# Moving the weight and token blocks of a Trainium2 transformer kernel to other starts within their 64-byte lines

## The chip, the cores and the metric

One core of one Trainium2 chip runs the kernel. The metric is the device time of one execution in microseconds (us); less is better.

## The reference

The reference is two transformer blocks on 512 tokens of width 1024 in float32. The first is a mixer (eight heads of forgetting attention beside four heads of gated linear attention), a cross attention to 256 memory tokens and an MLP of width 4096. The second has a gated MLP (ffn1), a token mixer with differential and block-sparse attention, and another gated MLP (ffn2). Cut to what matters here:

```python
def rms_norm(x, g):
    return x * rsqrt(mean(x * x) + EPS) * g
u = relu(rms_norm(h, norm_mlp_g) @ mlp_w1)          # the MLP: 1024 -> 4096 -> 1024
h = h + (u * u) @ mlp_w2
...
def swiglu(h, w1, w3, w2):                          # ffn1 and ffn2: 1024 -> 2816 -> 1024
    return (silu(h @ w1) * (h @ w3)) @ w2
x = x + 0.5 * swiglu(rmsnorm(x, ffn1_norm), w1, w3, w2)
```

## The kernel before

Every matrix product works on float32 values that are split into a high and a low part (names that end in `h` and `l`). One product is three matmuls: high by high, high by low, low by high. All activations lie transposed on chip, 128 partitions by tokens. A matmul has a stationary operand (128 columns, loaded first by a weight load) and a moving operand that streams through it.

Two kinds of dense work exist. A **panel** (`panel_t`, `chunks` and their kin, lines 975 to 977) takes 256 columns of a weight matrix for the whole depth of 1024. SyncE loads it into `raw`, ScalarE copies its high part into `wh`, VectorE subtracts the low part into `wl`. Its matmuls mostly stream 512 tokens, held in `xh`/`xl` or `ah`/`al`. The **products by sevens** do a part of the MLP and most of ffn1 and ffn2 with Strassen's scheme: a weight matrix and the tokens are cut into quarters, sums of quarters are formed, and seven block products take the place of eight. One block product is 24 matmuls (2 halves of columns, 4 slices of depth, 3 matmuls) with 256 moving columns each, accumulated in one bank. In the MLP it is the function `groups` (lines 1530 to 1532), in ffn1 and ffn2 the function `stream` (lines 1550 to 1552). TensorE runs them back to back in a fixed order; ScalarE, VectorE and the DMA queues prepare blocks ahead.

In these products the stationary operand is a weight block and the moving operand a token block:

- Weight blocks lie in halves of the sides of `wh`/`wl` (1024 floats each). In the MLP the slots 4 and 5 lie in the four quarters of `xh`, which holds no panel's tokens then (`parts_of`). In ffn1 and ffn2 a ring of five blocks is used (`ring_at`): four in `wh`/`wl`, and one, `RING_h`/`RING_l`, at the start of the arena.
- Token blocks are `XS_h`/`XS_l`, seven blocks of sums of the normed tokens in the arena, when the product goes up to the hidden width. When it goes down again (`DOWN`), they are the hidden values `US` in `xh`, `xl`, `ah`, `al` (`hidden_at`).

The arena is one large tensor, `arena` (and `arena_r`, the same bytes in the matmuls' type), in which the stages lay out what they need; the attentions' operands lie there too. Tensors are allocated one after another, so a tensor's length decides where the next one begins. In the built program the byte addresses within a partition are: `h` 2,176, `xh` 18,560, `xl` 34,944, `ah` 51,328, `al` 67,712, `raw` 84,096, `wh` 100,480, `wl` 116,864, `cst` (constants, with the identity matrix for transposes) 133,248, and `arena` 149,024. All but the arena's are multiples of 64; the arena begins 32 bytes past one. Slices of depth, halves of columns and blocks are multiples of 512 bytes apart, so a block's start tells the place in its line of all its matmuls.

Of the kernel before, what the change touches and what calls it, by code (L numbers as in the profile page):

```python
# [8 lines left out]
F32R = mybir.dt.float32r  # L9
AX = mybir.AxisListType  # L10

PART = 128
T, M, D = 512, 256, 1024
KT = D // PART
PC = 256
QT = T // PART
HALF = 64
D_FF, D_FF2 = 4096, 2816
CMP_L, CMP_S = 32, 16
NCMP = (T - CMP_L) // CMP_S + 1  # L20
# [7 lines left out]
W1_COL, at = {}, 0  # L28
# [3 lines left out]
W2_COL, at = {}, 0  # L32
# [5 lines left out]
P0, at = {}, 0  # L38
# [28 lines left out]
ROWS, at = {}, 0  # L67
# [40 lines left out]
HT = KT // 2  # L108
NETS = ["mlp", "ffn1", "ffn2"]
MLP_G = 6  # L110
PHASES, at = {}, 0
# [195 lines left out]
def constants():  # L307
# [4 lines left out]
    def put(name, a):  # L312
        nonlocal at
        a = np.asarray(a, np.float32).reshape(PART, -1)
        where[name] = at
        at += a.shape[1]
        parts.append(a)
# [13 lines left out]
    put("cmpany", (valid.any(-1)).astype(np.float32).T)  # L331
    put("tril", (p[:, None] % HALF) <= np.arange(HALF)[None, :])
    put("chunk", np.tile(np.arange(T)[None, :] % HALF != 0, (PART, 1)))
    put("block", (p[:, None] // HALF) == (p[None, :] // HALF))
    inv = (np.float32(1.0) / (np.float32(10000.0) ** (np.arange(0, HALF, 2, dtype=np.float32) / np.float32(HALF)))).astype(np.float32)
    ang = (np.arange(T, dtype=np.float32)[:, None] * inv[None, :]).astype(np.float32)
    put("cos", np.cos(ang).T[p % (HALF // 2)])
    put("sin", np.sin(ang).T[p % (HALF // 2)] * np.where(p % HALF < HALF // 2, -1.0, 1.0)[:, None])
    sel = np.zeros((PART, 4))
# [29 lines left out]
def build(nc, d, out):  # L369
    ctx = ExitStack()  # L370
    with ctx:
        def sb(name, shape, dt=F32):
            return ctx.enter_context(nc.sbuf_tensor(name, shape, dt))
# [6 lines left out]
        xh_at = -(-nc.sbuf_base // 32) * 32  # L380
        xh = sb("xh", [PART, KT, T], F32R)
        xh_f = nc.alloc_sbuf_tensor_at("xh_f", [PART, 4, HT, PC], F32, offset=xh_at)
        xl_at = -(-nc.sbuf_base // 32) * 32
        xl = sb("xl", [PART, KT, T], F32R)
        xl_f = nc.alloc_sbuf_tensor_at("xl_f", [PART, 4, HT, PC], F32, offset=xl_at)
# [4 lines left out]
        al = sb("al", [PART, KT, T], F32R)  # L390
        al_f = nc.alloc_sbuf_tensor_at("al_f", [PART, 4, HT, PC], F32, offset=al_at)
        raw = sb("raw", [PART, 2, KT, PC])
        wh = sb("wh", [PART, 2, KT, PC], F32R)
        wl = sb("wl", [PART, 2, KT, PC], F32R)
        cst = sb("cst", [PART, CONSTS.shape[1]])
        gT = sb("gT", [PART, NROWS])
        foxb = sb("foxb", [8, 1])
# [12 lines left out]
        std4 = sb("std4", [PART, QT])  # L410
        idle = sb("idle", [PART, 8])
        AW = 19936
        arena_at = -(-nc.sbuf_base // 32) * 32
        arena = sb("arena", [PART, AW])
        sm_h, sm_l = (x[:, 0, 0:KT * SMALL].rearrange("p (k n) -> p k n", k=KT) for x in (ah, al))
        arena_r = nc.alloc_sbuf_tensor_at("arena_r", [PART, AW], F32R, offset=arena_at)

        class Arena:
# [5 lines left out]
            def __call__(self, *shape):  # L424
                n = int(np.prod(shape))
                assert self.at + n <= AW, (self.at, n)
                v = self.store[:, self.at:self.at + n]
# [74 lines left out]

        A = Arena()
        N_sq, N_acc, N_dg = A(2, T), A(T), A(QT, PART)
        N_end = A.at
        F_out = A(KT, T)
        O_nat = A(QT, D)

        A = Arena()
        SM, PB, PTs = A(2, T), A(2, 2, T), A(2, T)  # L510
        att_end = A.at

        A = Arena(1024)
        A(T)
        X_h1, X_h2, X_std, X_inv, X_rs = (A(QT, 16) for _ in range(5))
        A = Arena(3072)
        H_sq = A(2, T)
        X_l = SM[0:16, 0, :]
        A = Arena(att_end)
# [13 lines left out]
        A = Arena(16300)  # L533
        G_dec = A(2, T // HALF)
        A = Arena()
        G_kn, G_at, G_S, G_sq = A(2, 2 * PART), A(2, 2, 2 * HALF), A(2, PART), A(4, PART)
        A = Arena(2048)
# [7 lines left out]
        A = Arena(att_end)  # L545
        A = Arena(att_end + 2 * T)
        M_sq, M_acc, M_dg = A(2, M), A(M), A(2, PART)
        N_rsm = M_sq[:, 0, :]
        A = Arena(att_end)
# [4 lines left out]
        A = Arena(16316)  # L554
        C_r2, C_ms, C_inv, C_rq, C_nrq = A(QT), A(QT), A(QT), A(4 * QT), A(4 * QT)

        A = Arena(N_end)
        XS_h, XS_l = (Arena(N_end + e * 7 * HT * PC, arena_r)(7 * HT, PC).rearrange("p (b k) n -> p b k n", b=7) for e in range(2))
        A = Arena(N_end + 2 * 7 * HT * PC)
        E_t, E_u, P_F = A(2, T), A(2, T), A(2, T)  # L560
        P_T = Arena(0)(4, PC)
        RING_h, RING_l = (Arena(e * HT * PC, arena_r)(HT, PC) for e in range(2))
        U_T = P_F.rearrange("p a n -> p (a n)").rearrange("p (a n) -> p a n", a=4)
        E_tl, E_tr, E_ul, E_ur = (e[:, c, :].rearrange("p (a n) -> p a n", a=2) for e in (E_t, E_u) for c in range(2))
        LEFT, RIGHT = slice(0, PC), slice(PC, T)
# [1 line left out]
        A = Arena(att_end)  # L567
# [12 lines left out]
        D_t = A(2, T)  # L580
        assert A.at <= AW, A.at

        S_x2 = arena[:, D_q[1].offset % AW:D_q[1].offset % AW + 4 * T].rearrange("p (a n) -> p a n", a=4)
        S_bf, S_kr, S_kraw, S_vT = SM, PTs, PB[:, 0], PB[:, 1]
        S_gT = D_on[:, 0].rearrange("p a n -> p (a n)")
        S_hT = D_on[:, 1].rearrange("p a n -> p (a n)").rearrange("p (a n) -> p a n", a=2)
        w2_at = D_V[1].offset % AW
        A = Arena(w2_at)
        S_w2k, S_w2v, S_h1 = A(2, PART), A(2, HALF), A(2, 2, 2 * NCMP)

        A = Arena(mix2_at)
# [29 lines left out]
        def parts_of(g, a):  # L621

            (net, r), i = PHASE_OF[g]
            slot = SLOT[PHASES[net, r][0], 7 * i + a]
            if slot < 4:
                return tuple(x[:, slot // 2, slot % 2 * HT:(slot % 2 + 1) * HT, :] for x in (wh, wl))
            x = xh.rearrange("p k n -> p (k n)").rearrange("p (b k n) -> p b k n", b=4, k=HT)
            return x[:, 2 * (slot - 4)], x[:, 2 * (slot - 4) + 1]

        def banks(g):  # L630

# [46 lines left out]
        def own(name):  # L678

            return (P0[name] + 10) % 2  # L680
# [9 lines left out]
        def ring_at(name, b):  # L690

            at = b % RINGS
            if at == 0:
                return RING_h, RING_l
            side = own(name) if at < 3 else 1 - own(name)
            at = (at - 1) % 2
            return tuple(x[:, side, at * HT:(at + 1) * HT, :] for x in (wh, wl))

        def landing(name, s, n):

# [269 lines left out]
        def _(pe):  # L970
# [542 lines left out]
            def groups(key):  # L1513

                g0 = PHASES[key][0]
                for i, n in TURN[key]:
                    g = g0 + i
                    a, b, at = PRODUCTS[n]
                    o = banks(g)[at].rearrange("p (f n) -> p f n", f=2)
                    (left_h, left_l) = parts_of(g, a)  # L1520
                    pe.wait_ge(st_l, high_count(g, a))
                    if n in (2, 4, 5):
                        pe.wait_ge(st_e, 3 * g + {2: 1, 4: 2, 5: 3}[n])
                    elif n == 6:
                        pe.wait_ge(st_c, 3 * g + 2)
                    for c in range(2):
                        cols = slice(c * PART, (c + 1) * PART)
                        for k in range(HT):
                            begins = n in (0, 1, 3) and c == 0 and k == 0
                            nc.tensor.matmul(o[:, c, :], left_h[:, k, cols], XS_h[:, b, k, :], start=begins, stop=False, skip_group_check=True)  # L1530
                            nc.tensor.matmul(o[:, c, :], left_h[:, k, cols], XS_l[:, b, k, :], start=False, stop=False, skip_group_check=True)
                            mm = nc.tensor.matmul(o[:, c, :], left_l[:, k, cols], XS_h[:, b, k, :], start=False, stop=k == HT - 1, skip_group_check=True)
                    mm.then_inc(st_q, 1)
# [343 lines left out]
        def _(act):  # L1877
# [458 lines left out]
            def block_high(g, a):  # L2336

                (net, r), i = PHASE_OF[g]
                g0, _, p = PHASES[net, r]
                n = 7 * i + a  # L2340
                if a in (A11, A12, A22):
                    act.wait_ge(st_r[buffers(g)], 48 * len(same_buffers(g)) + 48)
                else:
                    act.wait_ge(st_a, sum_count(g, SUM[a]))
                if n >= RING:
                    act.wait_ge(st_q, 7 * g0 + n - RING + 1)
                elif SLOT[g0, n] >= 4:
                    act.wait_ge(lin_done, 2 * (p - 4))
                else:
                    act.wait_ge(lin_done, 2 * (p - 1 if SLOT[g0, n] // 2 == p % 2 else p))  # L2350
                nc.scalar.activation(parts_of(g, a)[0], raw_of(g, BUF[a]), ACT.Copy).then_inc(st_h, 1)
# [434 lines left out]
        def _(dve):  # L2786
# [543 lines left out]
            def block_low(g, a):  # L3330

                dve.wait_ge(st_h, high_count(g, a))
                if a in SUM:
                    dve.wait_ge(st_a, sum_count(g, SUM[a]))
                to_h, to_l = parts_of(g, a)
                low(to_l, raw_of(g, BUF[a]), to_h, st_l)
# [711 lines left out]
```

## Time and profile before

| | |
|---|---|
| time before | 2123.26 us, median of 3 runs (2122.52 to 2123.94) |
| time of the profiled execution | 2123.62 us |
| its span, first to last instruction | 2121.8 us |
| TensorE busy | 2103.8 us (99%) |
| VectorE busy | 1399.6 us (66%) |
| ScalarE busy | 1053.1 us (50%) |
| granted TensorE clock | 1.000 of full speed |

The span is what the trace covers; the time of the execution is 1.82 us longer. Durations of matmuls overlap (one fills the array while the last one drains), so the pace of TensorE is not its duration of about 0.28 us but the distance from one start to the next. The timeline gives starts to 0.01 us, and 24 of them tell the pace of one block product.

### The profile page before, as it was taken

How to read it: one execution, taken by the hardware profiler on the slowest of the kernel's cores; microseconds unless marked ns; L12 is line 12 of the kernel's file. 1: busy time of each engine (PE TensorE's matmuls, PEld its weight loads, DVE VectorE, ACT ScalarE, POOL GpSimd, SP SyncE). 2: the span in 40 equal slices, each digit the busy share in tenths (PEclk: the TensorE clock that was granted, in tenths of full speed). 3: DMA queues.
4: the chain of work that ended last, by engine and by line, in shares of the span. 5: the costliest groups of instructions: out<-in, count | busy, mean ns of one | idle time of the engine just before them, and what ended most of it. 6: DMA issues, size and time to landing. Idle time of an engine off the chain costs nothing.

```text
span 2121.8 us, 33199 instructions
## 1 busy us (share of the span) xinstructions
PE 2103.8 (99%) x13292; PEld 1816.3 (86%) x13292; DVE 1399.6 (66%) x2337; ACT 1053.1 (50%) x1762; POOL 52.0 (2%) x68
## 2 busy tenths in 40 slices
PE   9999999999999999999999999999999999999999
PEld 7888988888998988899988888887777888899997
DVE  4664663467665767688856777647776357678874
ACT  6664545443533543464543565546667234445454
POOL 0000000000000011110100000000000000000000
PEclk9999999999999999999999999999999999999999
DMA  5121522156355366875543522321111233345432
GB/s 191 60 81 61 192 94 72 40 149 189 102 167 145 94 160 173 229 204 159 142 137 102 179 85 81 99 85 51 27 50 33 88 99 95 104 126 154 129 91 79
DMA packets 210827, 243.83 MB, mean 115 GB/s; under 512 B 9953, under 2 KB 193394, under 8 KB 210162
## 3 DMA queue, kind: packets, MB, share of 16 engines
q1 hardware_dynamic: 199410, 208.15, 31.1%
q0 software_dynamic: 11264, 33.56, 7.4%
q8 instruction: 106, 1.74, 0.3%
q14 instruction: 47, 0.39, 0.1%
HBM read 232.77 MB, written 35.65 MB: 127 GB/s over the span
## 4 chain that ended last, share of the span: by engine, by line
PE 95%; DVE 2%; ACT 1%; issue 1%; DMA 0%; SPq 0%; DVEq 0%; ACTq 0%
PE lin L975 19%; PE lin L977 19%; PE lin L976 19%; PE turned L1076 3%; PE score L1171 3%; PE score L1551 3%; PE score L1552 3%; PE mix L1552 3%; PE mix L1551 3%; PE score L1550 3%; PE mix L1550 3%; PE mix L1185 2%; PE turned L1552 1%; PE turned L1551 1%; PE turned L1550 1%; PE mix L1724 1%
## 5 line engine op out<-in xcount | busy, mean ns | idle before, releaser
L975 PE MATMUL lin<-xh,wh 128*128 128x512 f32 (+1 forms) x968 | 382.5, 395 | 1.7 <-DVE wl L2812 1.2
L977 PE MATMUL lin<-xh,wl 128*128 128x512 f32 (+1 forms) x968 | 369.9, 382 | 0.0
L976 PE MATMUL lin<-xl,wh 128*128 128x512 f32 (+1 forms) x968 | 368.8, 381 | 0.0
L975 PE MATMUL lin<-ah,wh 128*128 128x512 f32 x724 | 283.6, 392 | 1.4 <-DVE al L2817 0.6
L977 PE MATMUL lin<-ah,wl 128*128 128x512 f32 x724 | 281.1, 388 | 0.0
L976 PE MATMUL lin<-al,wh 128*128 128x512 f32 x724 | 280.9, 388 | 0.0
L2806 DVE TENSOR_TENSOR wl<-raw,wh 128x2048 fp32r<-128x2048 f32 x77 | 176.5, 2293 | 117.8 <-ACT wh L1890 117.8
L975 PEld LDWEIGHTS lin<-xh,wh 128*128 128x128 f32 x968 | 182.2, 188 | 43.0 <-issue 9.6
L977 PEld LDWEIGHTS lin<-xh,wl 128*128 128x128 f32 x968 | 182.0, 188 | 36.3
L976 PEld LDWEIGHTS lin<-xl,wh 128*128 128x128 f32 x968 | 182.5, 188 | 32.5 <-issue 1.0
L1890 ACT ACTIVATE wh<-raw 128x2048 fp32r<-128x2048 f32 x77 | 146.8, 1906 | 95.9 <-PE lin L977 80.7
L975 PEld LDWEIGHTS lin<-ah,wh 128*128 128x128 f32 x724 | 136.0, 188 | 30.8 <-issue 1.6
L977 PEld LDWEIGHTS lin<-ah,wl 128*128 128x128 f32 x724 | 135.9, 188 | 28.1
L976 PEld LDWEIGHTS lin<-al,wh 128*128 128x128 f32 x724 | 136.0, 188 | 27.7 <-issue 0.2
L2812 DVE TENSOR_TENSOR wl<-raw,wh 128x1024 fp32r<-128x1024 f32 x90 | 109.5, 1221 | 40.2 <-ACT wh L1897 39.6
L2920 DVE CUSTOM_DVE_ANT_0 arena<-score,cst 128x128 f32<-128x128 f32 (+2 forms) x224 | 97.6, 487 | 57.7 <-PE score L1171 46.6
L1975 ACT ACTIVATE arena<-turned 128x512 f32<-128x512 f32 (+1 forms) x128 | 68.9, 582 | 112.4 <-PE turned L1076 112.1
L1987 ACT ACTIVATE arena<-arena,negm 128x128 f32<-128x128 f32 (+2 forms) x224 | 122.9, 555 | 3.0 <-DVE negm L2920 3.0
L2817 DVE TENSOR_TENSOR wl<-raw,wh 128x1024 fp32r<-128x1024 f32 x84 | 102.3, 1221 | 26.5 <-ACT wh L2435 25.2
L1897 ACT ACTIVATE wh<-raw 128x1024 fp32r<-128x1024 f32 x90 | 94.1, 1053 | 35.5 <-PE lin L977 22.2
L2435 ACT ACTIVATE wh<-raw 128x1024 fp32r<-128x1024 f32 x70 | 73.9, 1056 | 66.6 <-PE score L1552 22.0
L1551 PE MATMUL mix<-arena_r,wh 128*128 128x256 f32 x320 | 89.5, 280 | 0.0
(563 smaller groups left out, 4735.9 us busy)
## 6 DMA issues: line engine op xcount, KB each, us to landing
raw<-in_w_in_dram SPq DMA_DIRECT2D x38, 1024.0 KB, 5.3
raw<-in_ffn_w_dram SPq DMA_DIRECT2D x46, 512.0 KB, 4.3
raw<-in_mlp_w_dram SPq DMA_DIRECT2D x20, 1024.0 KB, 5.6
raw<-in_ffn_w_dram SPq DMA_DIRECT2D x20, 1024.0 KB, 5.3
up_sums_ffn<-in_ffn_w_dram POOLq DMA_DIRECT2D x32, 512.0 KB, 5.4
down_sums_ffn<-in_ffn_w_dram POOLq DMA_DIRECT2D x24, 512.0 KB, 5.9
raw<-in_xattn_wkv_dram SPq DMA_DIRECT2D x8, 1024.0 KB, 5.3
raw<-in_w_out_dram SPq DMA_DIRECT2D x8, 1024.0 KB, 5.2
```

What stands on the lines that cost most here:

```text
L975: nc.tensor.matmul(o, w[0], x[0], start=first, stop=False)
L976: nc.tensor.matmul(o, w[0], x[1], start=False, stop=False)
L977: return nc.tensor.matmul(o, w[1], x[0], start=False, stop=last)
L1550: nc.tensor.matmul(o[:, c, :], left_h[:, k, cols], right_h[:, k, :], start=begins, stop=False, skip_group_check=True)
L1551: nc.tensor.matmul(o[:, c, :], left_h[:, k, cols], right_l[:, k, :], start=False, stop=False, skip_group_check=True)
L1552: mm = nc.tensor.matmul(o[:, c, :], left_l[:, k, cols], right_h[:, k, :], start=False, stop=k == HT - 1, skip_group_check=True)
L1890: nc.scalar.activation(wh[:, p % 2], raw[:, p % 2], ACT.Copy).then_inc(hi_done, 1)
L1987: op = nc.scalar.activation(PB[:, s % 2, a, col:col + nk], SM[:, a, col:col + nk], ACT.Exp, bias=negm[:, at:at + 1], scale=-1.0, accum_out ...
L2806: nc.vector.tensor_tensor(wl[:, p % 2], raw[:, p % 2], wh[:, p % 2].bitcast(F32), ALU.subtract).then_inc(conv_done, 1)
L2812: nc.vector.tensor_tensor(wl[:, p % 2, :, cols], raw[:, p % 2, :, cols], wh[:, p % 2, :, cols].bitcast(F32), ALU.subtract).then_inc(conv_d ...
L2817: nc.vector.tensor_tensor(dst, full, hi.bitcast(F32), ALU.subtract).then_inc(done, 1)
L2920: op = nc.vector.tensor_tensor_reduce(out=SM[:, a, col:col + nk], in0=ps[a][:, col:col + nk], in1=mask, scale=scale, scalar=BIG, op0=ALU.a ...
```

## The change

Offsets of the operands change, and no instruction is added, removed or moved: instruction by instruction all five engines' programs have the same order, operations, sizes and waits. What is new is where operands begin:

- A constant `SHIFT = 8` floats (32 bytes). The sides of `wh` and `wl` are 16 floats longer. Panels use them from the start of a side as before; the weight blocks of the products by sevens begin 8 floats in (`wh_blocks`, `wl_blocks`).
- The MLP's blocks in `xh` begin 8 floats in as well (`xh_blocks`), with 16 floats of room after `xh`.
- 8 floats are put before the arena; with the longer buffers ahead it now begins at 149,376, on a 64-byte line. `RING_h`/`RING_l` begin 8 floats into it, and `XS_h`/`XS_l` 16 floats later than before in it, so on a line.

As places in a 64-byte line (token operand, weight operand), the block products change so:

| block products | before | after |
|---|---|---|
| MLP, `XS` by `wh`/`wl` or `xh` | 32, 0 | 0, 32 |
| ffn1, ffn2: `XS` by `wh`/`wl` | 32, 0 | 0, 32 |
| ffn1, ffn2: `XS` by `RING` | 32, 32 | 0, 32 |
| ffn1, ffn2 down: `US` by `wh`/`wl` | 0, 0 | 0, 32 |
| ffn1, ffn2 down: `US` by `RING` | 0, 32 | 0, 32 |

Panels keep 0 for both. The other operands in the arena, of attention above all, go from 32 to 0. In lines of 128 bytes `xl`, `ah`, `al`, `raw`, `wh` and `wl` also move from 0 to 64, since the tensors before them are 64 or 128 bytes longer, while `h` and `xh` stay at 0.

```diff
+SHIFT = 8
...
         xh = sb("xh", [PART, KT, T], F32R)
         xh_f = nc.alloc_sbuf_tensor_at("xh_f", [PART, 4, HT, PC], F32, offset=xh_at)
+        sb("after_xh", [PART, 2 * SHIFT])
+        xh_blocks = nc.alloc_sbuf_tensor_at("xh_blocks", [PART, 4, HT, PC], F32R, offset=xh_at + 4 * SHIFT)
...
-        wh = sb("wh", [PART, 2, KT, PC], F32R)
-        wl = sb("wl", [PART, 2, KT, PC], F32R)
+        w_room = [sb(name, [PART, 2, KT * PC + 2 * SHIFT], F32R) for name in ("wh", "wl")]
+        wh, wl = (x[:, :, 0:KT * PC].rearrange("p s (k n) -> p s k n", k=KT) for x in w_room)
+        wh_blocks, wl_blocks = (x[:, :, SHIFT:SHIFT + KT * PC].rearrange("p s (b k n) -> p s b k n", b=2, k=HT) for x in w_room)
...
+        sb("before_arena", [PART, SHIFT])
         arena_at = -(-nc.sbuf_base // 32) * 32
...
-        XS_h, XS_l = (Arena(N_end + e * 7 * HT * PC, arena_r)(7 * HT, PC).rearrange("p (b k) n -> p b k n", b=7) for e in range(2))
-        A = Arena(N_end + 2 * 7 * HT * PC)
+        xs_at = N_end + 2 * SHIFT
+        XS_h, XS_l = (Arena(xs_at + e * 7 * HT * PC, arena_r)(7 * HT, PC).rearrange("p (b k) n -> p b k n", b=7) for e in range(2))
+        A = Arena(xs_at + 2 * 7 * HT * PC)
...
-        RING_h, RING_l = (Arena(e * HT * PC, arena_r)(HT, PC) for e in range(2))
+        RING_h, RING_l = (Arena(SHIFT + e * HT * PC, arena_r)(HT, PC) for e in range(2))
...
             if slot < 4:
-                return tuple(x[:, slot // 2, slot % 2 * HT:(slot % 2 + 1) * HT, :] for x in (wh, wl))
-            x = xh.rearrange("p k n -> p (k n)").rearrange("p (b k n) -> p b k n", b=4, k=HT)
-            return x[:, 2 * (slot - 4)], x[:, 2 * (slot - 4) + 1]
+                return wh_blocks[:, slot // 2, slot % 2], wl_blocks[:, slot // 2, slot % 2]
+            return xh_blocks[:, 2 * (slot - 4)], xh_blocks[:, 2 * (slot - 4) + 1]
...
-            return tuple(x[:, side, at * HT:(at + 1) * HT, :] for x in (wh, wl))
+            return wh_blocks[:, side, at], wl_blocks[:, side, at]
```

## Rows read from the trace of the kernel before

**Rows 1.** The profile's page: busy times, chain that ended last, two groups of instructions.
```profile
PE 2103.8 (99%) x13292; PEld 1816.3 (86%) x13292; DVE 1399.6 (66%) x2337; ACT 1053.1 (50%) x1762; POOL 52.0 (2%) x68
...
PE 95%; DVE 2%; ACT 1%; issue 1%; DMA 0%; SPq 0%; DVEq 0%; ACTq 0%
...
L975 PE MATMUL lin<-xh,wh 128*128 128x512 f32 (+1 forms) x968 | 382.5, 395 | 1.7 <-DVE wl L2812 1.2
...
L975 PE MATMUL lin<-ah,wh 128*128 128x512 f32 x724 | 283.6, 392 | 1.4 <-DVE al L2817 0.6
```
**Rows 2.** TensorE's matmuls of line 1550: count, duration min/median/max in ns, first and last start.
```profile
L1550 PE MATMUL mix<-arena_r,wh x320: 277/280/282, 896.5 to 2068.3; 128*128 128x256 f32 x160
L1550 PE MATMUL score<-arena_r,wh x304: 277/280/284, 885.2 to 2051.3; 128*128 128x256 f32 x152
L1550 PE MATMUL turned<-arena_r,wh x96: 277/280/283, 882.4 to 2054.2; 128*128 128x256 f32 x96
L1550 PE MATMUL score<-arena_r x80: 278/283/283, 879.5 to 2042.9; 128*128 128x256 f32 x80
...
L1550 PE MATMUL score<-xh,wh x48: 279/283/283, 958.7 to 1974.8; 128*128 128x256 f32 x48
...
L1550 PE MATMUL mix<-ah,arena_r x16: 279/282/286, 978.8 to 995.7; 128*128 128x256 f32 x16
```
**Rows 3.** The same view of line 1530, the products of the MLP.
```profile
L1530 PE MATMUL mix<-arena_r,wh x96: 277/281/283, 547.0 to 730.6; 128*128 128x256 f32 x96
```
**Rows 4.** Timeline of TensorE in ffn1: start us, duration us, line, output<-moving,stationary.
```profile
1001.77 0.28 PE L1550 MATMUL turned<-arena_r,wh 128*128 128x256 f32 x1
...
1004.59 0.28 PE L1550 MATMUL score<-arena_r,wh 128*128 128x256 f32 x1
...
1007.40 0.28 PE L1550 MATMUL score<-arena_r 128*128 128x256 f32 x1
...
1010.28 0.28 PE L1550 MATMUL score<-arena_r,wh 128*128 128x256 f32 x1
```
**Rows 5.** Timeline of TensorE in ffn1's down projection, columns as in rows 4.
```profile
973.06 0.28 PE L1550 MATMUL mix<-ah,wh 128*128 128x256 f32 x1
...
978.82 0.28 PE L1550 MATMUL mix<-ah,arena_r 128*128 128x256 f32 x1
...
979.54 0.28 PE L1550 MATMUL mix<-ah,arena_r 128*128 128x256 f32 x1
...
980.26 0.28 PE L1550 MATMUL mix<-ah,arena_r 128*128 128x256 f32 x1
...
981.69 0.28 PE L1550 MATMUL score<-ah,wh 128*128 128x256 f32 x1
```
**Rows 6.** Timeline of TensorE around the MLP's first 14 products, columns as in rows 4.
```profile
529.96 0.28 PE L1530 MATMUL score<-arena_r,xh 128*128 128x256 f32 x1
...
569.83 0.39 PE L975 MATMUL lin<-ah,wh 128*128 128x512 f32 x1
```
**Rows 7.** ScalarE's copies that fill the blocks in ffn1 and ffn2, columns as in rows 2.
```profile
L2435 ACT ACTIVATE wh<-raw x70: 1043/1060/1066, 871.6 to 2049.9; 128x1024 fp32r<-128x1024 f32 x70
L2435 ACT ACTIVATE arena_r<-raw x18: 1040/1050/1065, 883.1 to 2043.5; 128x1024 fp32r<-128x1024 f32 x18
```
**Rows 8.** Transposes whose stationary operand lies in h and in the arena, columns as in rows 2.
```profile
L1366 PE MATMUL turned<-cst,h x16: 272/273/273, 227.1 to 231.6; 128*128 128x128 f32 x16
...
L1076 PE MATMUL turned<-cst,arena x496: 272/273/331, 108.2 to 1637.2; 128*128 128x128 f32 x166
```
**Rows 9.** Timeline of TensorE in two panels of ffn2, columns as in rows 4.
```profile
1775.26 0.40 PE L977 MATMUL lin<-ah,wl 128*128 128x512 f32 x1
...
1777.34 0.39 PE L977 MATMUL lin<-ah,wl 128*128 128x512 f32 x1
...
1842.17 0.39 PE L975 MATMUL lin<-xh,wh 128*128 128x512 f32 x1
...
1844.21 0.39 PE L975 MATMUL lin<-xh,wh 128*128 128x512 f32 x1
```

More of the change, by code:

```diff
@@ L555, in build @@
         C_r2, C_ms, C_inv, C_rq, C_nrq = A(QT), A(QT), A(QT), A(4 * QT), A(4 * QT)
-        A = Arena(N_end)
-        XS_h, XS_l = (Arena(N_end + e * 7 * HT * PC, arena_r)(7 * HT, PC).rearrange("p (b k) n -> p b k n", b=7) for e in range(2))
-        A = Arena(N_end + 2 * 7 * HT * PC)
+        xs_at = N_end + 2 * SHIFT
+        XS_h, XS_l = (Arena(xs_at + e * 7 * HT * PC, arena_r)(7 * HT, PC).rearrange("p (b k) n -> p b k n", b=7) for e in range(2))
+        A = Arena(xs_at + 2 * 7 * HT * PC)
         E_t, E_u, P_F = A(2, T), A(2, T), A(2, T)
         P_T = Arena(0)(4, PC)
-        RING_h, RING_l = (Arena(e * HT * PC, arena_r)(HT, PC) for e in range(2))
+        RING_h, RING_l = (Arena(SHIFT + e * HT * PC, arena_r)(HT, PC) for e in range(2))
         U_T = P_F.rearrange("p a n -> p (a n)").rearrange("p (a n) -> p a n", a=4)
```

## The prediction

> **What bounds the kernel now.** First the page: TensorE is busy for 2103.8 of 2121.8 us and is 95% of the chain that ended last, while VectorE has 66% [rows 1]. So only TensorE's pace and its few stops count, and an edit that moves no instruction can act only by changing the pace. The duration of a matmul does not show it, since the next one starts before this one is over: 0.28 us stands in every row of the timeline. I therefore read the distance between starts. The list of line 1550 gives how many matmuls there are of each pair of operands [rows 2], the timeline gives the first start of successive block products, 24 matmuls apart [rows 4, 5], and the reader should put beside each pair where its two operands begin in their 64-byte lines (token, weight):
>
> - `XS` by `wh` (32, 0): 1001.77, 1004.59, 1007.40 are three first starts, so 5.63 / 2 = 2.815 us a product.
> - `XS` by `RING` (32, 32): 1007.40 to 1010.28, 2.88 us [rows 4].
> - `US` by `wh` (0, 0): 973.06 to 978.82 are two products, 2.88 us each [rows 5].
> - `US` by `RING` (0, 32): 978.82 to 981.69, 2.87 us; inside it 978.82, 979.54, 980.26 are six matmuls apart each time, 0.72 us, which is 2.88 us for 24 [rows 5].
> - the MLP's `XS` by `wh` or `xh` (32, 0): from the first start to the panel that follows, 529.96 to 569.83, lie 14 products: 39.87 / 14 = 2.848 us [rows 6].
>
> There is no stop in these stretches; each starts its next product one matmul's pace after the last. Two things stand out. The pace depends on the pair and not on the engine's partners: `RING` and `wh` are filled and read alike. And the pair (0, 32), which exists before in few products only, runs at 2.87 to 2.88 us and not at 2.815.
>
> **The change part by part.** No instruction is added, so every term is a number of products times a change of pace. Line 1550 is a third of a product's matmuls, so counts divided by 8 are products. `XS` by `wh`: 320 + 304 + 96 = 720, which is 90 products. `XS` by `RING`: 80 in the row shown and 96 in two more, 22 products. `US` by `wh`: six rows like the one shown hold 176, 22 products. `US` by `RING`: four rows hold 48, 6 products [rows 2]. The MLP's line 1530 has five rows, 336 in all (96 in the one shown), 42 products [rows 3]. Together 182.
>
> After the change all 182 are pairs (0, 32). The nearest row is the one that has just this pair, `US` by `RING`. I take its two readings as the two ends: 2.87 us, a whole product, and 2.88 us, its inner pace.
>
> - 90 products leave 2.815: 90 x 0.055 = +4.95 us to 90 x 0.065 = +5.85 us.
> - 42 MLP products leave 2.848: 42 x 0.022 = +0.92 us to 42 x 0.032 = +1.34 us.
> - 44 products (22 + 22) leave 2.88: 44 x -0.01 = -0.44 us to 0.
> - 6 products keep their pair: 0 to +0.06 us.
>
> The sum is +5.4 to +7.25 us; I take the middle, +6.3 us. TensorE is what everything waits for here, so nothing hides it.
>
> Edits that I cost at nothing. Panels keep both operands on a line, and matmuls on `wh` from a side's start are the same. The copies that fill blocks last the same whatever their target's place: 1060 ns to `wh` (on a line before) and 1050 ns to the ring (32 off) [rows 7]; if they lost 10 ns each it would be hidden, as these engines have slack. Attention's operands in the arena come onto a line: transposes with the stationary operand in `h` (on a line) and in the arena (32 off) both last 273 ns in the median [rows 8], and float32 pairs that are both in the arena stay equal to each other. I put that at 0, with 1 us either way.
>
> The profiled execution took 2123.62 us, so it should become 2123.6 + 6.3 = 2129.9 us; it lies 0.36 us above the median of 2123.26, which should become 2129.6 us, 0.30% more. I call less than 0.2% (4.25 us) no change, about what a measurement of this kernel can tell.
>
> A useful way to see it: before, the 182 products take 90 x 2.815 + 42 x 2.848 + 44 x 2.88 + 6 x 2.87 = 516.9 us, 2.840 us on average. All run at one new pace. Above 2.840 us the change loses, above 2.863 by over 0.2%, below 2.817 it wins by over 0.2%.
>
> **The rivals.**
>
> *Any two different places are fast.* The three slow kinds were two with equal places, and one might read the rows as "unequal is fast". Then `RING` and `US` products also run at 2.815: 44 x -0.065 + 6 x -0.055 = -3.2 us, 2120.1 us; if the MLP came down too, 42 x -0.033 = -1.4 us more, 2118.7 us. It decides as soon as the new pace is under 2.840. For it: the six products that contradict it follow products at 2.88 and may inherit a rhythm, and the MLP shows that one pair can hold two paces (2.848 and 2.815) depending on what went before. Against it: these six hold 0.72 us for every six matmuls without moving towards 0.70. Chance 0.17.
>
> *The MLP's pace everywhere.* If (0, 32) entered from panels settles at 2.848: 90 x 0.033 - 44 x 0.032 - 6 x 0.022 = +1.4 us, 2124.7 us. Chance 0.12.
>
> *The place in the line is not what sets the pace.* The fast pairs all have tokens in the arena and weights outside it; perhaps the tensors' distance counts. Then nothing changes, 2123.3 us. The Trainium skill speaks for this one: SBUF — State Buffer, in its specifications, gives lines of 16 bytes, of which 0 and 32 are both multiples, and TensorE: Matmul & The Clock Gate, under what happens when you issue a matmul, says that the moving operand and the weight load have read ports of their own and do not take bandwidth from each other. By these pages all five kinds would have one pace and the sum would be 0; the timeline shows 2.815 beside 2.88 with equal work, so they leave something out. The rows fit a cause in the places or in the tensors. Chance 0.05.
>
> *Lines of 128 bytes.* `xl`, `ah`, `al`, `wh` and `wl` move by 64, and no operand of a panel was there before. Panels are 968 + 724 matmuls of line 975 and as many of two more lines, some 5,000 [rows 1]. Their settled step is (1844.21 - 1842.17) / 9 = 0.2267 us, and after a stop it is (1777.34 - 1775.26) / 9 = 0.2311 us for a while [rows 9]. Should they no longer settle: 5,000 x 4.4 ns = +22 us. Should they gain as the block products did (0.065 / 24 = 2.7 ns): -13 us. Nothing in the profile speaks for either. Chance 0.05 slower, 0.03 faster.
>
> **How the numbers follow.** The forecast, the pace of the (0, 32) row, has 0.58; the rest as above. The likeliest case alone gives 2128.7 to 2130.5 us, with the 1 us of the arena 2128 to 2131. The range reaches down to the first rival and to 2131 above: 2119.8 to 2131.0, which leaves out the 128-byte cases and the first rival's lower half. Slower by over 0.2%: 0.58 + 0.05 = 0.63. Faster by over 0.2%: 0.03 and the first rival with the MLP in it, 0.05, together 0.08. Within 0.2%: 0.29.
>
> **What would show it.** In the trace after, first starts of block products of ffn1 should lie 2.87 to 2.88 us apart, with `wh` and with `RING` alike; the MLP's 14 products should take 40.2 to 40.3 us instead of 39.87; panels should keep 0.2267 us and the order of everything stays. Median durations of line 1550 should rise from 280 ns [rows 2] to about 282. The prediction is wrong if the 90 products keep 2.815, which would say that (0, 32) is no worse than (32, 0) and that the six products of before owed their pace to their neighbours, or if any other stage moves by more than 1 us.

## The result, and the profile after

The changed kernel takes 2136.22 us in the median (2135.88 to 2136.61, 6 runs) against 2123.05 us: a ratio of 1.0062, interval 1.0051 to 1.0072. It is slower by 13.2 us; 2129.6 us was forecast, and the range ended at 2131.0 us.

The head of the page after, and its rows of the two groups of panels that [rows 1] shows of before:

```profile
span 2134.5 us, 33199 instructions
...
PE 2118.5 (99%) x13292; PEld 1814.8 (85%) x13292; DVE 1399.9 (66%) x2337; ACT 1053.2 (49%) x1762; POOL 51.9 (2%) x68
...
L979 PE MATMUL lin<-xh,wh 128*128 128x512 f32 (+1 forms) x968 | 386.1, 399 | 1.6 <-DVE wl L2816 1.2
...
L979 PE MATMUL lin<-ah,wh 128*128 128x512 f32 x724 | 285.4, 394 | 1.1 <-DVE h L2871 0.5
```

TensorE is busy 14.7 us longer with the same 13,292 matmuls, VectorE and ScalarE are as they were, and the idle time before panels did not grow. So the pace changed, as forecast, but look at the durations: the panels' matmuls, which the change was said to leave alone, last 399 and 394 ns instead of 395 and 392.

Where did it go? The view of windows counts the matmuls of TensorE in a stretch; a count takes in the one or two that reach in from before, and TensorE does not stop in any of these. The stretches are, in this order, the MLP's products, ffn1's products before its down projection, its products after it, and panels. First the kernel before:

```profile
537.00:567.00 30.00, 30.00 (x256) 1.00 0.24 64
900.00:940.00 40.00, 40.00 (x342) 1.00 0.77 201
1010.00:1060.00 50.00, 50.00 (x427) 1.00 0.57 147
1660.00:1760.00 100.00, 100.00 (x443) 1.00 0.31 99
```

and the same view of the changed kernel:

```profile
537.00:567.00 30.00, 30.00 (x257) 1.00 0.31 88
900.00:940.00 40.00, 40.00 (x342) 1.00 0.71 191
1010.00:1060.00 50.00, 50.00 (x426) 1.00 0.58 151
1660.00:1760.00 100.00, 100.00 (x435) 1.00 0.30 95
```

The block products together do what they did; the panels do 8 matmuls less in 100 us. Less the two that reach in, a step is 100 / 441 = 0.2268 us before and 100 / 433 = 0.2309 us after. Summed over the whole trace, from each matmul's start to the next one's, panels with 512 moving columns take 1150.36 us before and 1168.03 us after (+17.7), panels with 256 columns 128.4 and 126.3 (-2.1), the MLP's products 119.6 and 118.6 (-1.0), those of ffn1 and ffn2 397.2 and 396.5 (-0.7), everything else on TensorE 318.5 and 317.3 (-1.2). That is +12.7 us, the growth of the span.

Within the products the terms cancel. First starts in ffn1 after the change, where [rows 4] has the same products:

```profile
1007.57 0.29 PE L1554 MATMUL turned<-arena_r,wh 128*128 128x256 f32 x1
...
1010.42 0.28 PE L1554 MATMUL score<-arena_r,wh 128*128 128x256 f32 x1
...
1013.26 0.28 PE L1554 MATMUL score<-arena_r 128*128 128x256 f32 x1
...
1016.06 0.28 PE L1554 MATMUL score<-arena_r,wh 128*128 128x256 f32 x1
```

`XS` by `wh` went from 2.815 to 2.85 and 2.84 us here (2.835 in the mean over both networks), `XS` by `RING` from 2.88 to 2.80 us (2.805 in the mean). And the MLP, forecast at 2.87 to 2.88 us:

```profile
549.51 0.28 PE L1534 MATMUL mix<-arena_r,wh 128*128 128x256 f32 x1
...
552.34 0.28 PE L1534 MATMUL score<-arena_r,xh_blocks 128*128 128x256 f32 x1
...
555.14 0.28 PE L1534 MATMUL turned<-arena_r,wh 128*128 128x256 f32 x1
...
557.97 0.29 PE L1534 MATMUL mix<-arena_r,wh 128*128 128x256 f32 x1
```

`XS` by `xh_blocks` takes 2.80 us, `XS` by `wh` 2.83. Both are the pair (0, 32), as is everything in ffn1, and yet the paces run from 2.80 to 2.85 us. So the two places in a 64-byte line alone do not set the pace.

### The profile page after: what moved, and what is told of

Same layout as the page of the kernel before. It is cut to its first block, busy times and chain, and to the rows that moved or that the text cites. A ratio compares the mean times of both kernels' runs of the same rounds, so it can differ in the third digit from the quotient of the medians.

```text
span 2134.5 us, 33199 instructions
## 1 busy us (share of the span) xinstructions
PE 2118.5 (99%) x13292; PEld 1814.8 (85%) x13292; DVE 1399.9 (66%) x2337; ACT 1053.2 (49%) x1762; POOL 51.9 (2%) x68
## 4 chain that ended last, share of the span: by engine, by line
PE 96%; DVE 2%; ACT 1%; issue 1%; DMA 0%; DVEq 0%; ACTq 0%
PE lin L979 19%; PE lin L981 19%; PE lin L980 19%; PE turned L1080 3%; PE score L1175 3%; PE score L1556 3%; PE mix L1556 3%; PE score L1554 3%; PE score L1555 3%; PE mix L1554 3%; PE mix L1555 3%; PE mix L1189 2%; PE turned L1556 1%; PE turned L1554 1%; PE turned L1555 1%; PE mix L1728 1%
## 5 line engine op out<-in xcount | busy, mean ns | idle before, releaser
L981 PE MATMUL lin<-ah,wl 128*128 128x512 f32 x724 | 285.8, 395 | 0.0
```

The costliest lines, as they stand in the source:

```text
L981: return nc.tensor.matmul(o, w[1], x[0], start=False, stop=last)
```

## Experiments

**Theory A.** What counts is the distance between the two operands, token start minus weight start, modulo some power of two above 64. Before, `xh`, `xl`, `ah`, `al`, `wh`, `wl` and their sides lie multiples of 8,192 bytes apart, so all panel operands have distance 0. The change puts 64 bytes after `xh` and 64 into each side of `wh` and `wl`, which makes the distances 0, -64, -128 and others, by tensor and side. (The text on the change says that `wh` and `wl` move from 0 to 64 in a 128-byte line. That is so for their first sides; the second sides lie another 64 further, at 0.) The rivals are named in the expectations.

**1. `pads_only`: the longer tensors without any shifted block.**

```diff
+        sb("after_xh", [PART, 16])
...
-        wh = sb("wh", [PART, 2, KT, PC], F32R)
-        wl = sb("wl", [PART, 2, KT, PC], F32R)
+        w_room = [sb(name, [PART, 2, KT * PC + 16], F32R) for name in ("wh", "wl")]
+        wh, wl = (x[:, :, 0:KT * PC].rearrange("p s (k n) -> p s k n", k=KT) for x in w_room)
```

> The change's longer tensors alone: 64 bytes after xh and 64 bytes more in each side of wh and wl; no block begins elsewhere in its side, and the arena still begins 32 bytes past a 64-byte line. Theory A (a panel's pace depends on where its two operands lie relative to each other beyond 64 bytes, and before they all lay exactly 16,384 bytes apart): the panels' 512-column steps rise from 0.2267 to about 0.230 us, the kernel comes out near 2139 us, since the gains of the block products are absent. Rival B (the loss comes from the new places of the blocks or of attention's operands in their 64-byte lines): 2123 us, no change.

Measured: 2142.12 us (2142.01 to 2142.56), ratio 1.0088, interval 1.0071 to 1.0104, so +18.4 us. Its panels in the view of windows:

```profile
1660.00:1760.00 100.00, 100.00 (x434) 1.00 0.26 85
```

That is the pace of the changed kernel (x435). Rival B falls: the padding alone costs more than the whole change, and what the change does to the blocks and the arena gives 5.9 us of it back (2142.12 to 2136.22). From start to start, the panels with 512 columns take 17.4 us more than before. The expectation was 3 us too low because it took the block products to stay as they were. Their distances moved with the padding too: those of ffn1 and ffn2 take 3.8 us more, those of the MLP 0.5 us.

**2. `gap64`, `gap512` and `all64`: one gap, in two places and two sizes.**

```diff
+        sb("gap", [PART, 16])                     # gap64; 128 floats in gap512
         raw = sb("raw", [PART, 2, KT, PC])
...
+        sb("ahead", [PART, 16])                   # all64, instead
         h = sb("h", [PART, KT, T])
```

> The kernel before with 64 bytes put between al and raw: all token tensors keep their distances to each other, wh, wl and the arena lie 64 bytes further away from them, everything stays at its place in a 64-byte line. Theory A: every panel step with 512 columns becomes slower, by 4 ns or more, 2143 us or more; XS by wh keeps 2.815 us a product, since both moved. Rival C (64-byte lines are all that counts, and the side length of wh with its 64 bytes did the harm): 2123 us.

> The same with 512 bytes. Theory A with a period of 512 bytes or less: as before, 2123 us, steps of 0.2267 us. Theory A with a longer period: slow panels as with 64 bytes.

> The kernel before with 64 bytes put ahead of h: every operand of TensorE moves by 64 bytes, all distances stay. Theory A (distances count): 2123 us. Rival D (the absolute place in a 128-byte line counts, and 64 is a bad one): slow panels, 2135 us or more.

Measured in one run each: 2142.98, 2124.18 and 2122.94 us. The panels of `gap64`, then of `gap512`, then of `all64`:

```profile
1660.00:1760.00 100.00, 100.00 (x430) 1.00 0.26 84
```

```profile
1660.00:1760.00 100.00, 100.00 (x443) 1.00 0.31 100
```

```profile
1660.00:1760.00 100.00, 100.00 (x443) 1.00 0.30 97
```

Moving everything by 64 bytes does nothing, so the absolute place in a 128-byte line does not count (rival D falls), and 64 bytes between tokens and weights cost as much as the padding, with sides as short as before (rival C falls). A gap of 512 bytes acts like none. `XS` by `wh`, both of which moved, keeps 2.816 us in ffn1 and ffn2, as expected. And `US` by `wh`, which `gap64` puts at -64 as well, ran faster, as these first starts show:

```profile
980.80 0.28 PE L1551 MATMUL score<-ah,wh 128*128 128x256 f32 x1
...
983.62 0.28 PE L1551 MATMUL mix<-ah,wh 128*128 128x256 f32 x1
...
986.45 0.28 PE L1551 MATMUL score<-ah,wh 128*128 128x256 f32 x1
```

2.83 us here, and 2.772 us in the mean of 18 such products, some at 2.72 and some at 2.83, where [rows 5] has 2.88. Distance 0, with 2.88 us among the slowest for 256 columns, is the best for 512.

**3. `minus64`: that distance for the products on `XS`, and nothing else moved.**

```diff
-        XS_h, XS_l = (Arena(N_end + e * 7 * HT * PC, arena_r)...
+        xs_at = N_end + 136
+        XS_h, XS_l = (Arena(xs_at + e * 7 * HT * PC, arena_r)...
...
-        RING_h, RING_l = (Arena(e * HT * PC, arena_r)...
+        RING_h, RING_l = (Arena(24 + e * HT * PC, arena_r)...
```

> The kernel before with only XS 544 bytes and RING 96 bytes later in the arena: modulo 512 the tokens then lie 64 bytes below each weight block, in wh, in RING and in xh alike; no panel operand moves. Theory A with a period of 512 bytes (US by wh ran at 2.772 us a product at that distance in the kernel with 64 bytes between al and raw): the 154 products on XS go from 2.816, 2.875 and 2.848 to about 2.77 us, 90 x 0.046 + 22 x 0.105 + 42 x 0.078 = 9.7 us less, 2113.5 us; panels keep 0.2267 us. Rival B (the place in the 64-byte line of each operand counts): the pairs are (0, 0), so 2.88 us a product, 2123 + 8 = 2131 us.

Measured: 2116.11 us (2115.82 to 2116.48), ratio 0.9967, interval 0.9954 to 0.9979. Rival B falls for good: all 154 products are pairs (0, 0), and they are faster. The size was missed by 2.6 us. The products on `XS` in ffn1 and ffn2 average 2.77 us, as forecast; the MLP's 42 stay at 2.827 us instead, which is 2.4 us. The windows show more:

```profile
537.00:567.00 30.00, 30.00 (x257) 1.00 0.22 56
900.00:940.00 40.00, 40.00 (x342) 1.00 0.76 205
1010.00:1060.00 50.00, 50.00 (x444) 1.00 0.62 159
1660.00:1760.00 100.00, 100.00 (x442) 1.00 0.30 95
```

The second and third stretch hold the same kinds of products with the same operands: 40 / 340 = 0.1176 us a step in one, 50 / 442 = 0.1131 in the other. From start to start a product takes 2.827 us in the MLP and ahead of the down projection, and 2.720 us behind it. One distance has two settled rhythms, and the 2.77 us is a mean of the two.

**4. A map of distances.** Five kernels with a gap before `raw` and `XS` shifted in the arena, each run once. The name gives both in bytes; the lengths in the diff are in floats and in the order of the expectations.

```diff
+        sb("gap", [PART, 8])                      # 8, 32, 112, 64, 120
...
+        xs_at = N_end + 8                         # 8, 16, 40, 32, 24
```

> A map of distances (token minus weight, modulo 512): 32 bytes between al and raw, XS 32 bytes later in the arena. Panels and US by wh at -32, XS by wh at -64, XS by RING at +32. Theory A: XS by wh about 2.77 us, XS by RING about 2.80 as after the change at that distance; panels slower than 0.2267 us. Rival B (unequal places in the 64-byte line are good): XS by wh, now (0, 32), at 2.835 us as after the change.

> The map: 128 bytes between al and raw, XS 64 bytes later. Panels and US by wh at -128, XS by wh at -32, XS by RING at +64. Theory A: panels near 0.233 us as at -64, unless 128 bytes is a period for them, then 0.2267; which of the two is the question.

> The map: 448 bytes between al and raw, XS 160 bytes later. Panels and US by wh at +64, XS by wh at +64, XS by RING at +160. If sign does not count, panels at 0.233 us and the products at 2.77 us as at -64; if it counts, another pace.

> 256 bytes between al and raw, XS 128 bytes later: panels and US by wh at 256, XS by wh at +32, XS by RING at +128. Theory A with a period of 256 bytes: panels 0.2267 and US by wh 2.88 us as at 0. With a period of 512: other paces.

> 480 bytes between al and raw, XS 96 bytes later: panels and US by wh at +32, XS by wh at 0, XS by RING at +96. Theory A: XS by wh falls to 2.88 us, the pace of equal places, though both operands keep the instructions they had; panels slower than 0.2267 us.

Measured: 2132.87, 2142.51, 2123.32, 2119.25 and 2150.70 us. The panels, in the order of the expectations, each from its own kernel:

```profile
1660.00:1760.00 100.00, 100.00 (x430) 1.00 0.29 95
```

```profile
1660.00:1760.00 100.00, 100.00 (x432) 1.00 0.26 84
```

```profile
1660.00:1760.00 100.00, 100.00 (x438) 1.00 0.30 95
```

```profile
1660.00:1760.00 100.00, 100.00 (x443) 1.00 0.30 95
```

```profile
1660.00:1760.00 100.00, 100.00 (x431) 1.00 0.29 95
```

256 bytes leave the panels at their best pace (and `US` by `wh` at 2.88 us), 128 do not: as far as 256 and 512 tell, the period is 256 bytes. And the products of `g480_x96` before ffn1's down projection, where `XS` by `wh` has come to distance 0, in the window that holds 342 matmuls in the kernel before:

```profile
900.00:940.00 40.00, 40.00 (x336) 1.00 0.74 207
```

All kernels together, with the time from the first start of a product to that of the next:

| distance | panel step, 512 columns (matmuls in 100 us) | block products, 24 matmuls with 256 columns |
|---|---|---|
| 0 (also 256, 512) | 0.2268 us (x443) | 2.88 us (`US` by `wh` before; `XS` by `wh` in `g480_x96`) |
| -32 | 0.2336 us (x430) | 2.84 us |
| -64 | 0.2336 us (x430) | 2.720 or 2.827 us |
| -96 | | 2.816 in ffn1 and ffn2; in the MLP 2.848 (before) or 2.88 (`XS` by `wh` in `gap64`) |
| -128 | 0.2326 us (x432) | 2.85 us |
| +64 | 0.2294 us (x438) | 2.720 or 2.827 us; `XS` by `RING` 2.75 in the mean of `g128_x64` |
| +32 | 0.2331 us (x431) | 2.80 and 2.81 us |
| +96 | | 2.87 us (`US` by `RING` before) |

Two expectations were missed in part. In `g32_x32` `XS` by `wh` ran at 2.724 us at -64, not 2.77 (and not at 2.835, so rival B falls there too). `g448_x160` shows that for panels +64 is not the mirror of -64, while the products have the same two paces at both. `g480_x96` behaved as theory A says: `XS` by `wh` at distance 0 fell from 2.816 to 2.88 us.

**5. `x32` and `x544_r480`: the faster mixtures, with panels untouched.**

```diff
+        xs_at = N_end + 8                         # x32: XS 32 bytes later, nothing else
...
+        xs_at = N_end + 136                       # x544_r480: XS 544 bytes later,
+        RING_h, RING_l = (Arena(120 + e * HT * PC, arena_r)...
```

> The kernel before with XS alone 32 bytes later in the arena, nothing else moved: XS by wh and by xh at a distance of -64 modulo 512, XS by RING at +32. Theory A: as in the kernel with 32 bytes before raw, which had the same two distances, XS by wh 2.724 and XS by RING 2.796 us a product; the MLP 2.83 us; panels 0.2267 us: 8.3 + 1.7 + 0.8 = 10.8 us less, 2112.4 us. Rival E (a pair's pace is its own, and 2.724 was an effect of other operands): 2.773 us as in the kernel that had -64 throughout, 2117 us.

> XS 544 and RING 480 bytes later: XS by wh and xh at -64 as before this run, XS by RING at +64, where it ran at 2.751 us. Theory A with paces that belong to the distance: about 1 us less than with RING at +32. If the products hand a rhythm on to those that follow, XS by wh leaves 2.724 us although its distance is the same.

Measured: `x32` 2112.14 us (2111.54 to 2112.22), ratio 0.9948, interval 0.9931 to 0.9964; `x544_r480` 2110.88 us (2110.78 to 2112.01), ratio 0.9943, interval 0.9928 to 0.9958. `x32` came out where theory A put it (2112.4), and rival E falls. The windows of `x32`:

```profile
537.00:567.00 30.00, 30.00 (x257) 1.00 0.20 56
900.00:940.00 40.00, 40.00 (x354) 1.00 0.80 216
1010.00:1060.00 50.00, 50.00 (x441) 1.00 0.64 166
1660.00:1760.00 100.00, 100.00 (x443) 1.00 0.29 95
```

and the two of `x544_r480` in ffn1:

```profile
900.00:940.00 40.00, 40.00 (x355) 1.00 0.78 216
1010.00:1060.00 50.00, 50.00 (x444) 1.00 0.64 168
```

Beside `minus64` the second stretch tells it: x354 and x355 where that kernel has x342, with `XS` by `wh` at -64 in all three. In ffn1 and ffn2 the four products after one on `RING` at another distance run at 2.720 us. In `x544_r480` they do so only from the second block on `RING` on: the first four by `wh` of each network still take 2.83 us, so the mean ahead of the down projections is 2.740 us. The distances are the same in both rounds, so something besides them counts, which may be what went before. There the products by `RING` at +64 come down to 2.720 us too, where `x32` has 2.796. The MLP, which has no `RING`, stays at 2.827 us in all three (x257). But `g32_x32` has a product with another distance in its MLP, `XS` by `xh` at -32 among those by `wh` at -64. These are the first starts of the same two products by `wh` in the first and in the second of the MLP's three groups of 14:

```profile
536.88 0.28 PE L1532 MATMUL turned<-arena_r,wh 128*128 128x256 f32 x1
...
539.71 0.28 PE L1532 MATMUL score<-arena_r,wh 128*128 128x256 f32 x1
...
621.33 0.28 PE L1532 MATMUL turned<-arena_r,wh 128*128 128x256 f32 x1
...
624.05 0.28 PE L1532 MATMUL score<-arena_r,wh 128*128 128x256 f32 x1
```

That is 2.83 us in the first group and 2.72 us in the second; the third has 2.83 us again. So a neighbour at another distance does not settle the rhythm by itself. Between `x32` and `x544_r480` the intervals do not decide. Both beat the kernel before and the change.

## Why the prediction was wrong, point by point

- **What bounds the kernel, and that only the pace can change:** right. All five engines' order stayed, the growth is on TensorE alone, and no stop was added.
- **The step that failed in sign and size is the cost of nothing put on "matmuls on `wh` from a side's start".** The panels with 512 columns paid +17.7 us, more than the whole result; those with 256 columns gave 2.1 us back. `pads_only`, which moves no block within its side, shows almost the same, +17.4 us. The fourth rival, "Lines of 128 bytes", had the place and the direction and priced it at +22 us; it was given 0.05, because "nothing in the profile speaks for either". That was true of the rows and false of the layout: every panel operand lay at the same address modulo 8,192, and a pace measured at one distance alone says nothing of another. It named the wrong quantity, absolute lines of 128 bytes (`all64` moves every operand by 64 and changes nothing) instead of distances modulo 256.
- **The terms of the block products** (+5.4 to +7.25 us) measured -1.7 us together. They rested on reading the five kinds of product as five pairs of places in a 64-byte line. The kinds differ in distance too: -96 for `XS` by `wh` and `xh`, 0 for `XS` by `RING` and for `US` by `wh`, +96 for `US` by `RING`. After the change no product keeps one of these distances throughout: with `XS`, the blocks on the first side have -32 for the high weights and +96 for the low ones, those on the second side -96 and +32, and `RING` and the MLP's `xh_blocks` have +32. The nearest row was thus a row of another distance. The last two kinds run at 2.80 us, the pace that +32 has in the map. `XS` by `wh` lost 0.019 us a product (+1.7 us for 90) instead of 0.055 to 0.065, `XS` by `RING` gained 0.070 (-1.5 us for 22) instead of 0.01, and the MLP gained 1.0 us instead of losing 1.
- **The third rival** said that the place in the line does not set the pace and that "perhaps the tensors' distance counts", and then gave no change, as if the edit left the distances alone. With the distances of the change worked out it would have asked for the panels.
- **The two readings of the Trainium skill** would have made all these layouts equal. SBUF — State Buffer, in its specifications, has lines of 16 bytes, and all starts here are multiples of that. TensorE: Matmul & The Clock Gate, under what happens when you issue a matmul, has read ports of their own for the moving operand and the weight load. The runs show 2122.94 us with all distances kept and 2142.98 us with 64 bytes between tokens and weights. So the two operands' places do bear on each other here; by what mechanism, no run shows.
- **The arena's other operands at nothing, with 1 us either way:** nothing here speaks against it. All that is neither panel nor block product changed by -1.2 us, just over that, but it did so in `all64` as well, whose layout moved as a whole and whose time stayed.
- The result stayed on the side to which most of the chance was given, but that was luck: the mechanism named for it brought a small gain.

## What to carry to other kernels

Work out, for every matmul whose operands a layout edit moves, the distance between its two operands before and after, modulo 256 bytes, and include those that "stay": padding one tensor changes the distance of all that lie behind it. Measure both widths on their own, since here the best distance for 512 moving columns is among the worst for 256. An edit that moves one operand alone, and leaves the panels at distance 0, was worth more than a scheme that moves many: `XS` later by 32 bytes gained 10.9 us (2123.04 to 2112.14), the change lost 13.2.

## What the runs showed of the hardware that was not expected

- Matmuls with weight loads between them have a pace that depends on the operands' distance with a period of 256 bytes, by up to 3% for 512 columns (0.2268 to 0.2336 us) and up to 6% for 256 columns (2.720 to 2.88 us for 24).
- One distance can have two settled rhythms. In `minus64`, with -64 throughout the products on `XS`, a product takes 2.827 us ahead of the down projection and 2.720 us behind it, and either holds for tens of us. At -96 the MLP has 2.848 or 2.88 us and ffn1 2.816 us. In `x544_r480` and in the MLP of `g32_x32` the pace of equal products changes from one round or group to the next. So the distance is not all, but what decides between the rhythms was not found, nor the mechanism under the period. Products that mix distances, as the change and `pads_only` have, were not mapped one by one. Whether padding by multiples of 256 bytes would save the change's own layout was not tried.
